# Branch A columns before branch B columns in the last projection group of the even cores

## The reference, cut to what matters

```
proj   = x @ w_in                 # 9728 columns: branch A q,k,v (3 groups), branch B q1,q2,k1,k2,v, two gates
y_a    = (3 dilated sliding-window attentions, 128 keys back at stride 1, 4, 16, merged by denominators) @ w_proj_a
y_b    = rms_norm(softmax(q1 k1) v - lambda softmax(q2 k2) v, causal over all keys) @ w_proj_b
x1     = layer_norm(alpha x + (sigmoid(g_a) y_a + sigmoid(g_b) y_b) @ w_out)
y      = layer_norm(alpha x1 + relu(x1 @ w_mlp1)^2 @ w_mlp2)
```

## Time and profile before

| | |
|---|---|
| time, median of 3 runs | 4661.69 us (4651.92 to 5232.98) |
| profiled execution | 4651.92 us, span of its slowest core (4) 4650.3 us |
| even cores 0, 2, 4, 6 | 4626.5, 4625.7, 4650.3, 4637.8 us |
| odd cores 1, 3, 5, 7 | 4535.7, 4528.4, 4563.2, 4531.6 us |
| TensorE busy on core 4 | 4362.6 us, 94% |
| ScalarE, VectorE, GpSimd busy | 55%, 39%, 18% |

### The profile page before, as it was taken

How to read it: one execution, slowest core, us unless ns; L and a number is a source line. 1 busy time by engine, 2 the same in 40 slices (tenths; PEclk the granted TensorE clock), 3 DMA queues, 4 the chain that set the end, 5 groups by cost and what they waited for, 6 DMA issues and landing times.

```text
span 4650.3 us, 99774 instructions; the slowest of 8 cores (4528.4 to 4650.3 us)
## 1 busy us (share of the span) xinstructions
PE 4362.6 (94%) x37400; PEld 2469.2 (53%) x37400; DVE 1794.0 (39%) x3795; ACT 2570.3 (55%) x3263; POOL 856.0 (18%) x1113
## 2 busy tenths in 40 slices
PE   7798999899999999998889999999999999999998
PEld 3344444444445555555444665755656557556565
DVE  1655645522122322227414342253342533424353
ACT  1465556611156666668766566665665665666510
POOL 2000003311100000004312213123031130220322
PEclk9999999999999999999999999999999999999999
DMA  8664447988775555567857465365573664745363
GB/s 141 157 167 109 114 123 204 257 205 192 139 140 133 124 128 123 120 152 206 236 149 191 136 186 152 124 194 152 165 197 122 179 178 133 198 139 159 100 205 123
DMA packets 554461, 738.48 MB, mean 159 GB/s; under 512 B 165250, under 2 KB 352770, under 8 KB 552066
## 3 DMA queue, kind: packets, MB, share of 16 engines
q1 hardware_dynamic: 448450, 449.91, 34.8%
q0 software_dynamic: 105536, 282.11, 25.3%
HBM read 630.15 MB, written 191.87 MB: 177 GB/s over the span
## 4 chain that ended last, share of the span: by engine, by line
PE 76%; DMA 8%; DVE 6%; ACT 4%; issue 3%; SPq 2%; POOL 0%; DVEq 0%; ACTq 0%; POOLq 0%
PE PSB L638 45%; PE PSB L1381 19%; PE PSB L1353 11%; ACT m_PT_44 L424 1%; SPq L208 1%; DMA m_WR_147<-wp 1%; SPq L203 1%; DMA VA<-m_VAS_86 1%; DMA m_CB_107<-AO 1%; DVE m_OO_50 L1423 1%; ACT m_PTF_163 L424 1%; DVE m_TT_49 L1418 1%; DMA SG<-m_FST_78 1%; ACT m_PT_43 L424 1%; DMA m_KB_114<-KTB 1%
## 5 line engine op out<-in xcount | busy, mean ns | idle before, releaser
L424 ACT ACTIVATE m_PT_43<-PSB 128x1024 bf16<-128x1024 f32 x544 | 556.2, 1022 | 578.0 <-PE PSB L1353 447.5
L424 ACT ACTIVATE m_PT_45<-PSB 128x1024 bf16<-128x1024 f32 (+1 forms) x544 | 530.1, 975 | 554.4 <-PE PSB L1353 468.5
L424 ACT ACTIVATE m_PT_44<-PSB 128x1024 bf16<-128x1024 f32 (+1 forms) x544 | 540.7, 994 | 0.0
L424 ACT ACTIVATE m_PT_46<-PSB 128x1024 bf16<-128x1024 f32 (+1 forms) x544 | 514.6, 946 | 2.4 <-DVE PSB L1365 1.7
L1353 PE MATMUL PSB<-m_QB_69,m_KB_114 64*128 64x512 bf16 (+1 forms) x672 | 108.2, 380 | 44.3 <-DMA m_KB_114<-KTB 20.6
L1365 DVE TENSOR_TENSOR PSB<-PSB,m_BT_71 128x512 f32<-128x512 f32 (+1 forms) x156 | 86.3, 590 | 123.9 <-PE PSB L1353 123.6
L638 PE MATMUL PSB<-m_X1A,m_WR_146 128*128 128x512 bf16 x512 | 121.9, 379 | 2.3 <-DVE m_T_178 L1070 1.9
L638 PE MATMUL PSB<-m_X1A,m_WR_149 128*128 128x512 bf16 x512 | 122.7, 379 | 0.9 <-issue 0.2
L638 PE MATMUL PSB<-m_X1A,m_WR_147 128*128 128x512 bf16 x512 | 121.0, 379 | 2.5 <-DVE m_T_177 L1070 2.2
L638 PE MATMUL PSB<-m_X1A,m_WR_148 128*128 128x512 bf16 x512 | 120.7, 379 | 1.1 <-DVE m_T_176 L1070 0.8
L208 POOL DMA_DIRECT2D m_WR_146<-wp x48 | 27.1, 577 | 456.0 <-PE PSB L1353 230.0
(11 more groups left out here) (871 smaller groups left out, 10149.9 us busy)
## 6 DMA issues: line engine op xcount, KB each, us to landing
m_WR_146<-WB POOLq DMA_DIRECT2D x84, 512.0 KB, 6.1
m_WR_147<-WB POOLq DMA_DIRECT2D x84, 512.0 KB, 6.5
m_WR_148<-WB POOLq DMA_DIRECT2D x84, 512.0 KB, 6.1
m_WR_149<-WB POOLq DMA_DIRECT2D x84, 512.0 KB, 6.3
WB<-wm POOLq DMA_DIRECT2D x84, 256.0 KB, 12.8
m_VB_118<-VB SPq DMA_DIRECT2D x68, 258.0 KB, 4.5
m_VB_120<-VB SPq DMA_DIRECT2D x68, 258.0 KB, 4.8
m_KB_114<-KTB SPq DMA_DIRECT2D x68, 256.0 KB, 4.3
```

The source lines that it names most:

```text
L424: return self.P.op("scalar", lambda e: e.activation(out=out, in_=in_, func=func, bias=bias, scale=scale), 165.0 + 0.861 * n, rd, wr, gen)
```

## The change

In the last projection group of type 0 the nine units of A come ahead of the six of B0. Nothing else in the text of the program changes; the planner lays out the even cores' order anew from it.

```
--- before.py
+++ after.py
@@ -540,7 +540,7 @@
             pl = [("P", (0, 1, 2, 3), B0 + A + GT, ()), ("P", (4, 5, 6, 7), KV, ()), ("P", (8, 9, 10, 11), KV + DUP, ()),
-                  ("P", (12, 13, 14, 15), B0 + A + GT, (11,))]
+                  ("P", (12, 13, 14, 15), A + B0 + GT, (11,))]
         else:
```

## The result

The kernel after took 4708.62 us, median of four runs (4698.83 to 4714.35); its profiled execution 4706.67 us. The ratio to the kernel before is 1.0109, 95% interval 1.0074 to 1.0144: some 51 us slower on 4651.92 us, 1.1%, with an interval clear of 1. The forecast was +22.

The account below looks back on a forecast made before the run. TensorE on the even cores was taken to bound nearly everything, so only its idle time could move; -5 - 7 + 4 + 30 - 5 + 5 = +22 us on 4651.92 gave 4674 us, range 4622 to 4735.

Parts of the forecast that it names:

- Order: Even cores: dense stretch grows by 201 us, second branch A run right behind the first, then all heads of tiles 12 to 15.
- The second run, -5: Second branch A run: fillers that VectorE may empty too replace gates, easing ScalarE; -5 us, between 0 and -16.
- The bound of -16: Most the second branch A run could gain, if it shrank to the first run's 154 us.
- The start of the heads, -7: After the dense stretch: the 7.3 us wait for first keys goes; -7 us, between -7 and 0.
- the longer dense stretch, +4: Dense stretch: nine added branch A units bring some stalls; +4 us, between 0 and 21.
- that rival: Clock rival: a lower clock share through the new dense stretch, 4687 us at 0.94, 4720 at 13/16; chance 0.03.
- The thinner mix, +30: Attention steps of tiles 12 to 15: 117 fewer fill jobs at 0.26 us each; +30 us, between 0 and 80.
- the test that I had set, idle time a step: Mixed stretches: if idle time per step is unchanged, the +30 for fewer fills among attention steps is wrong.
- The free mix: Rival: fewer fills among attention steps cost nothing as jobs are split; 4634 us, chance 0.25.
- the full price (+80): Rival: jobs stay whole and each missing one leaves a step held by ScalarE; +80, 4724 us, chance 0.14.
- The casts, +5: First tile's M1 and M2: sixteen weights cast late on POOL, nearly hidden by a four-weight lead; +5 us, 0 to +14.
- Starting O1, -5: O1's start: waits for gates remain, but freed from the run's last stores it may lose less; -5, between 0 and -15.

Follow-up runs that it names:

- odd cores' experiment: Kernel before, with the odd cores' last group taking branch A columns ahead of branch B's, even cores' order kept; ratio 0.998.
- long dense kernel: Kernel before, order of columns kept, but even cores run fills alone until 6656 are left ahead of tile 12's first head; profiled 4683.16 us, no ratio.
- casts early: Kernel after, but the last group casts weights again while branch A loads are next in line, so also in the dense stretch; ratio 1.0132.
- in the mix: Kernel after, but units of the last group after its twelfth cast one more weight every fifth job, among heads; ratio 1.004.

## Why the prediction was right or wrong

*Order.* Right: run at 1517 to 1687 (forecast 1490 to 1655), O1 at 2173 (2100), 376 fills in the run (330), less than the 500 that would have refuted the reading of the run.

*The second run, -5.* Sign right, size -13, reason wrong. I credited jobs emptied by VectorE as well. The odd cores' experiment and the long dense kernel give the same gain with the gates still in the run: it came from no longer running beside the odd cores' run. I had read one core's trace, and the odd cores' run stands in no row that I looked at; so "odd cores unchanged" was wrong too. The bound of -16 was not sound either: the first run, whose 154 us I took for the same work, has 600 QK matmuls of branch A, the second 768.

*The start of the heads, -7, and the longer dense stretch, +4.* Their sum of -3 was -6. The wait of the earlier trace rows did go. The clock was granted 0.98 in the dense stretch before and after, nearly all of it at the upper of the two levels (2.4 GHz); one window, 1230 to 1260 us, had 0.77, where it had 0.94 before. So that rival did not occur. Its "1.00 throughout" was a misreading: the earlier trace rows give 0.99 for the second long mixed stretch.

*The thinner mix, +30.* It was +40 in the two stretches by loss. But 11 to 17 of it are the gates' Tanh, which I took out of the run in one term and never put down where they went. Without them the thin mix is some +23 to +29 in this kernel; in the long dense kernel, whose gates stand as before, it is +42. This spread I did not resolve. By the test that I had set, idle time a step, the +30 would have been called wrong; some 20 us of the second stretch of core 4 sit in longer QK matmuls instead, and the test was badly chosen. The free mix fell, and the full price (+80) too.

*The casts, +5, and Starting O1, -5: the step that failed.* Together forecast at 0, measured at **+32**: +12 in O1 and O2 up to the first M1, +4 in M1, +16 in the first M2. The mechanism was the one named (load behind cast on POOL), and the lead held through M1. In the first M2 it ran out: TensorE stood 12.0 us for weights there on the mean of the even cores, as much as a deficit of 72 us leaves over a lead of 60. I called that nearly hidden and priced it as steps that go on without fills, at up to 0.68 us each. TensorE stood still instead, and behind those waits its clock fell to the lower level for a time: 0.96 was granted in the first M2, where it had been 1.00. "Starting O1" was priced as if it stood clear of the casts. The sixth weight is cast at 2256 us in the middle of it, and the casts early and in the mix both bring O1 and O2 back to 26 to 28 us of loss, from 39, where the kernel before has 27. How these 12 us divide I can only argue: 3 us more for weights, 3 for products, 4 for exponentials, and a clock granted 0.90 from 2173 to 2330 us.

So range and sign held, though the run's gain was luck, its cause being another. By these terms the sum was off by -8 (run), -3 (dense and start of the heads), +10 (mix) and +32 (casts and O1), together +31. With the 5 us ahead of the change that is the 36 between the mean even core's 58 and the forecast 22.

## What to carry to other kernels

When a reordering removes the slots in which background work was issued, count the work that is now late, and price what the lead does not cover as time in which the busiest engine stands still, not as a thinner mix. Follow every instruction taken out of one stage to the stage where it lands, and read the neighbouring cores' windows at the same time as the one studied: who shares the memory with whom changes when a stage moves. Background transfers belong where the DMA engines are half idle: the same sixteen weights' casts cost some 30 us late, some 35 early, and nothing among the heads.

## What the runs showed of the hardware

*Runs of neighbouring cores.* With cores 4 and 5 both in their branch A runs, each at a DMA share near 0.9, they moved 261 and 247 GB/s and the even cores' runs lost 50.2 us on the mean; with core 5 at 104 GB/s core 4 moved 283 and they lost 35.1. All eight cores' runs coincide before, so that the pair alone does this was not tried. The Trainium skill (HBM Reference, Specifications) says that the two cores of a pair share about 716 GB/s, some 358 each when both stream. Both cores here were at about 250, under that share, and the slower run is still measured.

*Casts beside dense fills.* With 13 weights cast in the dense stretch and three in the run, these lost 22 and 13 us more than with none; among heads at a DMA share of 0.47 the same casts cost less than the spread between runs.

*Clock behind a wait.* On core 4 of the kernel after the granted level fell from the upper to the lower one during or right behind TensorE's waits of 15.2 us in O1 and of 6.3 and 4.3 us in the first M2; in M1, without such a wait, 1.00 was granted throughout.

*Busy and held.* Four QK matmuls show 0.88 us in place of 0.61 in steps without fills, with no idle time marked before them. That they are held by their score banks is read from the steps; no run measured it by itself.
